# Rotary exchange of partition halves by DMA instead of a TensorE product, in a two-model transformer kernel on one core

## The reference

```python
def rope(x, positions):              # dilated layer: halves of 32 within a head of 64
    x1, x2 = jnp.split(x, 2, axis=-1)
    return jnp.concatenate([x1 * c - x2 * s, x2 * c + x1 * s], axis=-1)

def apply_rope(x, cos, sin):         # neighbourhood layers: even and odd elements of a head
    x1, x2 = x[..., 0::2], x[..., 1::2]
    y = jnp.stack([x1 * c - x2 * s, x1 * s + x2 * c], axis=-1)
    return y.reshape(x.shape)
```

## Time and profile before

| | |
|---|---|
| median of 3 runs | 1998.01 us (1995.0 to 1999.14) |
| profiled execution | 1994.43 us, span 1992.6 us |
| TensorE busy | 1946.0 us, 98% |
| VectorE busy | 1291.2 us, 65% |
| ScalarE busy | 913.6 us, 46% |
| GpSimd busy | 168.9 us, 8% |
| DMA | 317.49 MB, mean 159 GB/s |

### The profile page before, as it was taken

One profiled execution on the slowest core, in us unless ns is written; L12 is line 12 of the kernel. 1 busy time (PEld: TensorE's weight loads), 2 busy tenths in 40 slices (PEclk: granted clock), 3 DMA queues, 4 the chain that ended last, 5 costly groups with the idle time before them and its releaser, 6 DMA issues.

```text
span 1992.6 us, 32294 instructions
## 1 busy us (share of the span) xinstructions
PE 1946.0 (98%) x13021; PEld 1675.6 (84%) x13021; DVE 1291.2 (65%) x2272; ACT 913.6 (46%) x1596; POOL 168.9 (8%) x187
## 2 busy tenths in 40 slices
PE   8999999999999999999999999999999999999998
PEld 7869888898798888887688887888888998998887
DVE  6765677777557777535434447767667745677776
ACT  5655654545566555424523334322232536455443
POOL 0220000002103200003510000000000012000000
PEclk9999999999999999999999999999999999999999
DMA  7365598855747665314533323455556431664554
GB/s 240 103 212 170 151 235 226 224 174 163 235 147 192 190 217 160 117 56 151 141 100 108 100 87 116 139 175 164 185 189 195 135 92 57 187 195 148 178 182 137
DMA packets 313322, 317.49 MB, mean 159 GB/s; under 512 B 17079, under 2 KB 291398, under 8 KB 312918
## 3 DMA queue, kind: packets, MB, share of 16 engines
q1 hardware_dynamic: 308156, 301.65, 49.3%
q0 software_dynamic: 3904, 12.03, 2.8%
q10 hardware_dynamic: 1114, 1.76, 0.3%
HBM read 306.54 MB, written 8.85 MB: 158 GB/s over the span
## 4 chain that ended last, share of the span: by engine, by line
PE 86%; DVE 7%; ACT 3%; DMA 1%; issue 1%; POOL 0%; ACTq 0%; DVEq 0%; POOLq 0%
PE acc L697 16%; PE acc L699 16%; PE acc L698 16%; PE acc L747 15%; PE acc L746 7%; DVE w_low L2043 3%; PE acc L743 2%; PE pss L929 2%; PE pst L941 1%; ACT w_high L1489 1%; PE acc L712 1%; PE acc L744 1%; PE acc L819 1%; PE acc L956 1%; PE acc L713 1%
## 5 line engine op out<-in xcount | busy, mean ns | idle before, releaser
L2043 DVE TENSOR_TENSOR w_low<-raw,w_high 128x1024 fp32r<-128x1024 f32 (+4 forms) x503 | 560.6, 1155 | 125.1 <-ACT w_high L1489 122.8
L1489 ACT ACTIVATE w_high<-raw 128x1024 fp32r<-128x1024 f32 (+4 forms) x503 | 471.6, 985 | 329.9 <-PE acc L699 181.8
L697 PE MATMUL acc<-normed,w_high 128*128 128x512 f32 (+2 forms) x1096 | 375.0, 342 | 0.4 <-DVE w_low L2043 0.3
L699 PE MATMUL acc<-normed,w_low 128*128 128x512 f32 (+2 forms) x1096 | 370.6, 338 | 0.0
L698 PE MATMUL acc<-normed,w_high 128*128 128x512 f32 (+2 forms) x1096 | 370.5, 338 | 0.0
L747 PE MATMUL acc<-normed,w_high 128*128 128x512 f32 x840 | 299.2, 396 | 0.0
L746 PE MATMUL acc<-normed,w_low 128*128 128x256 f32 x840 | 234.7, 279 | 1.1 <-DVE normed L2069 1.0
L697 PEld LDWEIGHTS acc<-normed,w_high 128*128 128x128 f32 (+1 forms) x1096 | 207.6, 189 | 26.0 <-issue 2.0
L699 PEld LDWEIGHTS acc<-normed,w_low 128*128 128x128 f32 (+1 forms) x1096 | 207.6, 189 | 22.3
L698 PEld LDWEIGHTS acc<-normed,w_high 128*128 128x128 f32 (+1 forms) x1096 | 207.7, 189 | 22.1
L747 PE MATMUL acc<-inner,w_high 128*128 128x512 f32 x612 | 218.2, 396 | 0.0
(11 more groups left out here) (287 smaller groups left out, 2937.0 us busy)
## 6 DMA issues: line engine op xcount, KB each, us to landing
raw<-in_w_ff SPq DMA_DIRECT2D x128, 512.0 KB, 4.3
raw<-in_w_mod SPq DMA_DIRECT2D x96, 512.0 KB, 4.5
raw<-in_w_in SPq DMA_DIRECT2D x84, 512.0 KB, 4.0
raw<-in_l_w_gate SPq DMA_DIRECT2D x44, 512.0 KB, 5.2
raw<-in_l_w_up SPq DMA_DIRECT2D x44, 512.0 KB, 4.6
raw<-in_l_w_down SPq DMA_DIRECT2D x32, 512.0 KB, 4.6
raw<-in_l_w_qkv SPq DMA_DIRECT2D x24, 512.0 KB, 4.5
raw<-in_l_w_out SPq DMA_DIRECT2D x16, 512.0 KB, 4.7
```

The lines of the kernel that those rows point to most:

```text
L697: mm(dst, lh, rh, start=i == 0, stop=False)
L699: ins = mm(dst, ll, rh, start=False, stop=i == n - 1)
L1489: nc.scalar.activation(WH[:, s % NSPLIT, w0:w0 + nw], RAW[:, r:r + nw], ACT.Copy).then_inc(w_high, 1)
L2043: V.tensor_tensor(WL[:, s % NSPLIT, c], RAW[:, r:r + nw], WH[:, s % NSPLIT, c].bitcast(F32), ALU.subtract).then_inc(w_low, 1)
```

## The change

TensorE no longer turns the blocks of the dilated and neighbourhood layers. Instead ScalarE issues, for each block, four copies from SBUF to SBUF into one of two halves of a second buffer, `OTHER` (the first two banks of `probs_t`, which the attentions use later). Each copy moves 32 partitions with rows of 2 KB. For the dilated layer a copy takes a block of 32 partitions to the block beside it; for the neighbourhood layers it takes every second partition of a half to its neighbours. VectorE reads `OTHER` for the sine product, and GpSimd waits for the copies (`exchanged`) before its cosine product, since it works in place. The exchange itself has no signs; they are put into the sine tables, and for `rot64`, which the sliding-window layer goes on using, into the frequencies.

```diff
-            rot64[h * 64 + j, h * 64 + 32 + j] = -1.0
+            rot64[h * 64 + j, h * 64 + 32 + j] = 1.0
...
-    put("sin_axial", np.sin(ang))
+    put("sin_axial", np.sin(ang) * np.tile([-1.0, 1.0], P // 2)[:, None])
...
+        OTHER = [view(PT, BANK * i, (2, S)) for i in range(2)]
...
# TensorE, dilated, then neighbourhood
-                            rotate(dil_raw[i - 2:i - 1], const("rot64"), "dil", out[i - 2])
+                            st["rope"] += 1
...
-                        rotate(na_raw(T)[i - 1:i], const("rot_axial"), f"na{l}",
-                               st["acc"] - 1 - (len(banks(2, T)) if i < 2 else 2))
+                        st["rope"] += 1
...
# GpSimd, before its cosine product
+                    if name:
+                        pool.wait_ge(acc_full, g + 1)
+                    else:
+                        n = st["swaps"]
+                        st["swaps"] += 1
+                        pool.wait_ge(exchanged[n % 2], 64 * (n // 2 + 1))
...
# ScalarE
+            def exchange(raw, g, blocks):
+                n = st["swaps"]
+                st["swaps"] += 1
+                act.wait_ge(acc_free[g % 4], g // 4 + 1)
+                if n > 1:
+                    act.wait_ge(rope_done, 8 + n - 1)
+                dst = OTHER[n % 2]
+                for lo in range(4):
+                    to = slice(32 * lo, 32 * lo + 32) if blocks else slice(64 * (lo // 2) + lo % 2, 64 * (lo // 2) + 64, 2)
+                    at = 32 * (lo ^ 1) if blocks else 64 * (lo // 2) + (lo % 2 ^ 1)
+                    of = slice(at, at + 32) if blocks else slice(at, 64 * (lo // 2) + 64, 2)
+                    act.dma_start(dst[to], raw[of]).then_inc(exchanged[n % 2], 16)
...
-                    split(3)
+                    split()
+                    exchange(dil_raw[0], g, True)
+                    for i in range(1, 3):
+                        split()
+                        exchange(dil_raw[i], g + 1 + i, True)
                     for i in range(4):
                         highs(mem_chunks()[i:i + 1])
                         split()
-                    split()
-                    st["acc"] += 13
+                        exchange(dil_raw[3 + i], g + 4 + i, True)
+                    split()
+                    exchange(dil_raw[7], g + 8, True)
+                    st["acc"] += 7
...
                     split()
-                    st["acc"] += i
+                    exchange(na_raw(T)[i], st["acc"] - 1, False)
...
                     split()
-                    st["acc"] += 1
+                    exchange(na_raw(T)[2 + i], st["acc"] - 1, False)
...
# VectorE
+            def rope_exchanged(r, sinv):
+                n = st["swaps"]
+                st["swaps"] += 1
+                dve.wait_ge(stored, st["store"])
+                tmp = TMP[:, 0, :].rearrange("p (a n) -> p a n", a=2)
+                dve.wait_ge(exchanged[n % 2], 64 * (n // 2 + 1))
+                link(V.tensor_tensor(tmp, OTHER[n % 2], sinv(r), ALU.mult))
+                st["rot"] += 1
+                dve.wait_ge(rot_done, st["rot"])
+                turned(V.tensor_tensor(r, r, tmp, ALU.add))
```

More of the change, by code:

```diff
@@ L34 @@
 for _name, _width in (("ident", 128), ("ones", 128), ("spread", 512), ("rot64", 128), ("rot_mla", 128),
-                      ("rot_axial", 128), ("window", 256), ("cos_axial", 256), ("sin_axial", 256), ("freq64", 1),
+                      ("window", 256), ("cos_axial", 256), ("sin_axial", 256), ("freq64", 1),
                       ("freq_mla", 1)):
@@ L82, in constants @@
     put("rot_mla", rot_mla.T)
[L83 to L87, removed]
     col = np.arange(64)
@@ L98, in constants @@
     put("cos_axial", np.cos(ang))
-    put("sin_axial", np.sin(ang))
+    put("sin_axial", np.sin(ang) * np.tile([-1.0, 1.0], P // 2)[:, None])
     inv32 = (np.float32(10000.0) ** (-np.arange(0, 64, 2, dtype=np.float32) / np.float32(64))).astype(np.float32)
-    put("freq64", np.tile(inv32, 4)[:, None])
+    put("freq64", np.concatenate([-inv32, inv32, -inv32, inv32])[:, None])
     inv16 = (np.float32(10000.0) ** (-np.arange(0, 32, 2, dtype=np.float32) / np.float32(32))).astype(np.float32)
@@ L546, in build @@
         rope_done = sem("rope_done")
+        exchanged = [sem(f"exchanged{i}") for i in range(2)]
         bias_done = sem("bias_done")
@@ L1316, in _ @@
                 attention(na_tasks(l), 0 if l else MODS, lead=lambda: values(1, blocks=[0, 1, 2, 3]), tail=gate_tail,
-                          keys=st["acc"] - 3, ropes=st["rope"] - 1)
+                          keys=st["acc"] - 2, ropes=st["rope"] - 1)
                 if l == 0:
@@ L1389, in _ @@
         def _(pool):
-            st = {"phase": 0, "rot": 0, "task": 0, "acc": 0}
+            st = {"phase": 0, "rot": 0, "task": 0, "acc": 0, "swaps": 0}
             go = lambda: fence(pool, st)
@@ L1412, in rope @@
             def rope(raw, cosv, name):
-                for g, r in zip(rotated[name], raw):
-                    pool.wait_ge(acc_full, g + 1)
+                for g, r in zip(rotated[name] if name else raw, raw):
+                    if name:
[4 more added lines that the diff above has]
+                        pool.wait_ge(exchanged[n % 2], 64 * (n // 2 + 1))
                     nc.gpsimd.tensor_tensor(r, r, cosv(r), ALU.mult).then_inc(rot_done, 1)
@@ L1450, in _ @@
             skew()
-            rope(dil_raw, cos64, "dil")
+            rope(dil_raw, cos64, None)
             attention(dil_tasks)
@@ L1459, in _ @@
                 bias(l)
-                rope(na_raw(2 * S if l == 0 else S), cos_axial, f"na{l}")
+                rope(na_raw(2 * S if l == 0 else S), cos_axial, None)
                 attention(na_tasks(l))
@@ L1465, in _ @@
             st = {"phase": 0, "chain": 0, "acc": 0, "task": 0, "sig": 0, "split": 0, "store": 0, "res": [], "lot": 0,
-                  "pair": 0, "roots": 0, "steps": 0}
+                  "pair": 0, "roots": 0, "swaps": 0, "steps": 0}
             go = lambda: fence(act, st)
@@ L1788, in v_lead @@
                         split()
-                        st["acc"] += i < 2
                     for i in range(3):
@@ L1918, in na_lead @@
                     split()
-                    st["acc"] += i == 0
                 na_lead(0)
@@ L2015, in _ @@
             st = {"phase": 0, "chain": 0, "acc": 0, "task": 0, "rot": 0, "sig": 0, "split": 0, "store": 0, "mod": 0,
-                  "relu": 0, "turned": 0, "spread": 0, "added": 0, "known": 0}
+                  "relu": 0, "turned": 0, "spread": 0, "added": 0, "known": 0, "swaps": 0}
             go = lambda: fence(dve, st)
@@ L2531, in _ @@
                         if i > 1:
-                            rope(dil_raw[i - 2:i - 1], sin64)
+                            rope_exchanged(dil_raw[i - 2], sin64)
                         if 2 <= i < 6:
@@ L2673, in _ @@
                     if i:
-                        rope(na_raw(T)[i - 1:i], sin_axial)
+                        rope_exchanged(na_raw(T)[i - 1], sin_axial)
                 st["acc"] += 2
```

## The result

The changed kernel is **slower by 0.35%**: 2004.4 us median (10 runs) against 1997.09 us for the kernel before (10 runs), ratio 1.0035 with a 95% interval of 1.0026 to 1.0045. Forecast was 1993.9 us, with 1986 to 2000.5 for 8 in 10. Its profiled execution took 2003.87 us, with a span of 2002.1 us, 9.5 us more than before.

A forecast was written before the change was run, and what follows sets the result against it. TensorE, busy for 98% of the span, was taken as the bound. Neighbourhood layers -7.0 us and dilated layer +2.9 us gave -4.1 us, from a median of 1998.01 to 1993.9 us; range 1986 to 2000.5 for 8 in 10.

The forecast's parts named there:

- Part 2: ScalarE's queue: four copies issued per rotary block at 0.352 us each plus gaps, 1.53 us; bounds 1.02 and 2.43 us.
- rival (b): ScalarE's queue: back-to-back issues cost 2.43 us or more per block, total +3.7 us, 2001.7 us; chance 0.09.
- Part 3: Dilated layer's order: issues delay the memory norm's copy, VectorE's lap grows to 7.71 us, stage ends 2.9 us later.
- U10: A late weight unit (v) of the dilated projections on TensorE; forecast to start at 479.1 us, before at 476.2.
- U3: An early weight unit of the dilated projections on TensorE; forecast to start at 429.8 us, before at 429.87.
- R0: End of VectorE's first rotary sum in the dilated layer, later sums numbered onward; forecast 435.3 us, before 435.22.
- Part 4: VectorE and GpSimd: sine product from the second buffer costs 0 us more; landing hidden, 11.7 us allowed, 6.8 for the first.
- Part 1: TensorE: removing 16 rotary products at 0.87 us can win 13.9 us, 7.0 dilated and 7.0 neighbourhood.
- Part 5: Neighbourhood layers: issues and landing fit in existing room, so eight products x 0.87 us win 7.0 us.
- (a): ScalarE's queue: issue is cheap, below 1.1 us per block, total -7.2 to -11 us, 1987 to 1991 us; chance 0.32.
- (c): Transfers: exchanges land far behind the weight stream and hold VectorE; at 14 us landing, 18 us, 2012 us; chance 0.05.
- (d): Attention behind the neighbourhood layers: softmax sets the pace, -7.0 becomes about -3, total near 0, 1998 us; chance 0.12.

The follow-up runs named there:

- x1: Changed kernel with one plain-copy DMA per dilated block in place of four, same bytes, partner exchange left out; ratio 0.9976 to the kernel before.
- x_no_cosine: Changed kernel with GpSimd's cosine product in the dilated layer cut to one column of each half; 1999.01 us, ratio 1.001 to the kernel before.
- e1: Changed kernel with the dilated layer's rotary products back on TensorE, exchanges only in the neighbourhood layers; 1988.77 us, ratio 0.9967 to the kernel before.
- e3: Changed kernel with each dilated exchange put behind the next memory copy and w_high in ScalarE's order; 1986.78 us, ratio 0.9959 to the kernel before.
- e4: Changed kernel, same order, with eight dilated exchange buffers for two, so no exchange waits for a sum; 1987.98 us, ratio 0.9963 to the kernel before.

## Why the prediction was wrong

**The step that failed is the price of an issue in Part 2.** I took 4 x 0.352 us and gaps, 1.53 us per block, from ScalarE's output store, and put 0.09 on rival (b), back-to-back issues at the price of the w_pool loads. Rival (b)'s price came: the first of four takes about 0.5 us and the following ones 0.61, with a median of 614 ns against the 596 of the w_pool loads, so 2.44 to 2.69 us per block, and 3.31 for the first block. My reason against it, that the nearest row is the one most like it in memory and row length, weighed the wrong likeness. The rows do not show why the lone store is cheaper. Of the rows that I took, only the w_pool one is of four issues with no wait between them. In x1 a single issue of the store's size, 256 KB, took 472 ns against the store's 352, so being one of a series is part of the price and not all of it.

**The term in the sum.** Part 3 at 2.43 us per block gave U10 at 486.9, 10.7 us late. Redone by its own steps, that walk gives less: first exchange to 427.2, U3 at 430.6, R0 436.1, four laps of 8.61 to R4 470.5, R5 478.2 and w_low of U10 at 485.3, so 9.1 us late. Measured were 13.6 (14.4 from the copy of `pst`). Two things were missing. The first is at the head of the stage, where the forecast let U3 start unchanged at 429.8:

```profile
423.99 3.31 ACTq L1527 DMA_DIRECT2D probs_t<-work  x4
427.40 1.06 ACT L1490 ACTIVATE w_high<-raw 128x1024 fp32r<-128x1024 f32 x1 [9.11 <-issue]
```

The first exchange took 3.31 us, 0.9 more than 2.43, and the next six together 0.5 more than at 2.43. The second is VectorE. The walk had taken each w_low pair at its old 2.8 us, and had priced the sine product out of SBUF at nothing (Part 4), because the sum beside it, also with two SBUF operands, took 0.69 us. Where it met GpSimd's product, the sine product took 1.78 us:

```profile
443.39 1.78 DVE L2311 TENSOR_TENSOR probs_t<-probs_t,rope 128x512 f32<-128x512 f32 x1
```

The added collisions above are 3.4 us. Together 9.1 + 0.9 + 0.5 + 3.4 = 13.9 us, near what was measured. I had named these collisions only as a possible gain (up to 3.5 us, if they fell into idle time); they grew. The cosine product starts when the transfers land, which is now inside VectorE's w_low and sine product.
The Trainium skill, page "Advanced Engine Details and Errata", section "GPSIMD Details", says that GpSimd shares a read and a write interface with VectorE and conflicts with its instructions that have two inputs in SBUF. The 1.78 us beside GpSimd and the 0.68 without it agree. It speaks against moving the sine product's operand out of PSUM, and I had not weighed it. The trace of the kernel before shows the other form, the sine product with its operand in PSUM, beside GpSimd's product over its whole length, and neither is slowed:

```profile
907.78 0.69 DVE L2294 TENSOR_TENSOR probs_t<-acc,cst 128x512 f32<-128x512 f32 x1 [7.45 <-PE acc L912]
907.79 1.28 POOL L1415 TENSOR_TENSOR work<-work,cst 128x512 f32<-128x512 f32 x1 [11.07 <-PE acc L912]
```

The same pair stands at 1635.60 us.

**Rival (b)'s total.** It said 2001.7, and 2004.4 was measured, or 1.0035 where 2001.7 would be 1.0018 of 1998.01. Between its +3.7 us and the +9.5 of the spans lie 5.8 us. U10 has 2.9 of them (13.6 in place of 10.7), accounted for above. The rest is the 3 us from the first scores (+13.5) to the end of the layer (+16.5). There the trace shows a wait of TensorE for the weights w_mod of 2.3 us, 0.8 before, and a granted clock of 0.89 between 515 and 530 us, 1.00 before. I changed neither by itself, so that they are the cause of these 3 us is read, not tested. In x_no_cosine that wait is 0.6 us and the clock 1.00, and its +9.7 at the first scores is +9.5 at the end of the layer: the addition is not there. The wait for w_mod is not the change's own, for it is also longer in e1 (1.9 us, with +1.4 from the first scores to the memset), whose dilated part is that of the kernel before.

**Parts that held.** Part 1: 64 instructions of TensorE are gone. Part 3's mechanism: the copy is held behind the issues and the lap grows by what they outlast its old wait; e3 and e4 each show it by taking one leg away. Part 4, landing: 2.1 us median against the 11.7 us allowed, VectorE's sine product waited for a transfer once, 2.3 us at the last block of neighbourhood layer 0, where TensorE was busy throughout (59.00 of the 59 us from 870). The prediction had named such a wait as a sign of being wrong; this one cost nothing. Part 5: -3.6 and -3.4 us, together the 7.0 forecast. It holds at the higher price too: TensorE stays busy there, so nothing that it needs is held behind the issues for long enough to matter. So rivals (a), (c) and (d) did not come.
The Trainium skill, page "DMA: Bandwidth & Descriptors", section "Anatomy of one DMA — SWDGE (gpsimd) path", gives about 50 ns for the sequencer's dispatch and a fixed cost near 2 us, for DMAs issued from GpSimd. The exchanges are issued from ScalarE, which that section does not cover. Their landing of 2.1 us lies near its second figure; its first is no price for ScalarE's queue, which was held for 614 ns per issue.
The rule of the Trainium skill against splitting a transfer over partitions (page "DMA: Bandwidth & Descriptors", section "Rules for kernel authors") is borne out here by the table: one issue is 0.0059 of the time cheaper than four, though by the issues and not by the engines' bandwidth.

**The clock.** TensorE's granted clock falls after some of these waits, and not after others. First four windows of the changed kernel, then two of x_no_cosine:

```profile
430.00:440.00 10.00, 8.02 (x54) 8.02 (x55) 7.29 (x9) 2.74 (x4) 2.45 (x2) 0.83 0.80 240
440.00:450.00 10.00, 10.00 (x85) 10.00 (x85) 7.09 (x9) 3.05 (x4) 2.36 (x1) 1.00 0.49 142
450.00:460.00 10.00, 7.22 (x49) 7.02 (x48) 7.34 (x11) 3.62 (x5) 1.29 (x1) 0.83 0.46 131
470.00:480.00 10.00, 6.51 (x53) 6.11 (x51) 6.93 (x7) 2.00 (x2) 3.99 (x2) 1.00 0.48 133
```

```profile
430.00:440.00 10.00, 7.84 (x66) 7.64 (x65) 7.14 (x9) 3.79 (x5) 2.12 (x2) 1.00 0.81 244
450.00:460.00 10.00, 6.32 (x51) 5.91 (x49) 7.34 (x11) 3.21 (x4) 0.89 (x2) 1.00 0.44 131
```

1.00 is the level of 2.4 GHz, and 0.83 a mean of it and of 1.2 GHz. In windows of 2 us the changed kernel is at 0.50, the level of 1.2 GHz, in 434 to 436, 454 to 456, 464 to 466 and 482 to 484, shortly after waits of 3.48, 2.78, 1.82 and 3.55 us, and stays at 1.00 after those of 0.81 and 1.44. But x_no_cosine stays at 1.00 after two waits of 2.16 us and falls after one of 2.11. So the idle time of a 10 us window or the length of a single wait doesn't tell whether it falls, and what does is left open here. My sum had no term for the clock. As VectorE sets the lap there, the lower clock mostly fills time in which TensorE would have waited; this is read from the rows, not tested.

## What to carry to other kernels

Before a DMA is put in a compute engine's queue, count its issues times the dearest price that the trace shows for several in a row, and ask what stands behind them: the same four issues cost nothing behind the next copy and w_high, and ahead of them held VectorE for 2 us more in each lap. A wait for a buffer at the head of the issues turned most of their duration into delay; eight buffers in place of two, or a later place in the queue, undid it. And where an operand moves from PSUM to SBUF, ask again which of the other engine's instructions it will meet: out of PSUM the product took 0.69 us beside GpSimd's, out of SBUF up to 1.78.

## What the runs showed of the hardware

- Between issue and compute on ScalarE there can be overlap: in e3 the issues at 444.81 to 447.24 run while the copy and w_high run. They hold up only what stands behind them in program order, and in the neighbourhood layer of the changed kernel too two of them (877.04, 1.35 us) lie beside w_high (876.91, 1.05 us).
- An issue of such a copy within SBUF holds ScalarE's queue for 472 to 614 ns (medians), with 32 to 256 KB behind it: least where it is alone (472), and 586 to 614 where two, four or eight follow each other.
- A VectorE product or sum with both operands in SBUF, 128x512 in f32, takes 0.68 us alone and 1.66 to 1.79 us beside a GpSimd product over 128x512, while one with an operand in PSUM takes 0.69 beside it; a pair of w_low (two of 128x1024) takes 2.35 us alone and up to 3.44.
